# A transformer-and-SSD pipeline on one core: norms written by feature pairs, and the value projection moved to the front of its group

## What is computed

```python
# layer 2, its end
h = rms_norm(x, mlp_norm[1]);  x = x + (relu(h @ w_in) ** 2) @ w_out        # "mlp1", hidden width 4096
# hybrid layer
sh1, sc1, g1, sh2, sc2, g2 = split(silu(c) @ ada_w + ada_b, 6)              # and sh1c, sc1c from c_ctx
h  = rms_norm(x,   norm1_w) * (1 + sc1)  + sh1                              # "hx"
hc = rms_norm(ctx, norm1_w) * (1 + sc1c) + sh1c                             # "hc", 256 context tokens
p  = h @ w_in            # columns: q, k, v, z (512 each), xs 512, bc 512, dt 16
kvc, sc_in = hc @ w_in[:, 512:1536], hc @ w_in[:, 2048:]
# rope on q and k, neighbourhood attention with the context's keys and values,
# convolution and SSD scan of xs, B, C with dt, gated by silu(z)
x = x + g1 * (concat(attn, y_ssd) @ w_out_2)                                # "out"
h = rms_norm(x, norm2_w) * (1 + sc2) + sh2                                  # "m2"
x = x + g2 * ((silu(conv(h @ up_gate)) * (h @ up_val)) @ w_down)            # "glu", 22 tiles of 128
return rms_norm(x, final_norm_w)
```

## Time and profile before

| | |
|---|---|
| median of 3 runs | 1223.09 us (1213.04 to 1224.58) |
| profiled execution, its own time | 1223.84 us |
| its span in the trace | 1221.7 us |
| TensorE matmul busy | 1077.3 us, 88% |
| VectorE busy | 734.6 us, 60% |
| ScalarE busy | 538.5 us, 44% |
| mean granted TensorE clock | 0.923 of full |

### The profile page before, as it was taken

One profiled execution on the slowest core, in us unless ns is written; L12 is line 12 of the kernel. 1 busy time (PEld: TensorE's weight loads), 2 busy tenths in 40 slices (PEclk: granted clock), 3 DMA queues, 4 the chain that ended last, 5 costly groups with the idle time before them and its releaser, 6 DMA issues.

```text
span 1221.7 us, 15756 instructions
## 1 busy us (share of the span) xinstructions
PE 1077.3 (88%) x6140; PEld 923.2 (76%) x6140; DVE 734.6 (60%) x996; ACT 538.5 (44%) x726; POOL 96.9 (8%) x71
## 2 busy tenths in 40 slices
PE   3786899998998988999999979898889677999995
PEld 2574689888887866889999769776436567999994
DVE  5556566898745555757766555532456546566564
ACT  3455446564424555544555326323332034444442
POOL 0002002675000010000000000000000000000000
PEclk8878999999989998999999979988786688999998
DMA  4343256676732551457776412420100042545431
GB/s 163 105 141 105 81 212 235 237 270 230 257 142 104 183 195 69 172 207 272 280 277 236 175 70 75 143 104 24 73 1 1 1 155 91 195 164 205 174 152 52
DMA packets 29007, 184.05 MB, mean 151 GB/s; under 512 B 3472, under 2 KB 5008, under 8 KB 9360
## 3 DMA queue, kind: packets, MB, share of 16 engines
q1 hardware_dynamic: 23360, 153.82, 34.4%
q0 software_dynamic: 3456, 25.17, 5.7%
q10 hardware_dynamic: 2144, 4.42, 1.5%
HBM read 180.77 MB, written 2.62 MB: 150 GB/s over the span
## 4 chain that ended last, share of the span: by engine, by line
PE 52%; issue 21%; DVE 13%; ACT 6%; DMA 1%; POOL 1%; DVEq 0%; POOLq 0%; ACTq 0%; SPq 0%
PE bank L579 13%; PE bank L580 13%; PE bank L581 13%; DVE split L1548 4%; ACT split L1081 4%; PE bank L588 2%; PE bank L1007 2%; PE bank L981 2%; PE bank L965 1%; PE bank L807 1%; DMA raw<-w_mlp 1%; PE bank L993 1%; POOL stat L518 1%; PE bank L744 1%; ACT work L1137 1%
## 5 line engine op out<-in xcount | busy, mean ns | idle before, releaser
L1548 DVE TENSOR_TENSOR split<-raw,split 128x2048 fp32r<-128x2048 f32 (+2 forms) x133 | 300.0, 2256 | 293.8 <-ACT split L1081 288.2
L1081 ACT ACTIVATE split<-raw 128x2048 fp32r<-128x2048 f32 (+2 forms) x133 | 247.6, 1862 | 352.3 <-PE bank L581 306.2
L579 PE MATMUL bank<-acts,split 128*128 128x256 f32 (+1 forms) x1024 | 292.3, 285 | 12.6 <-DVE acts L1578 12.3
L580 PE MATMUL bank<-acts,split 128*128 128x256 f32 (+1 forms) x1024 | 291.7, 285 | 0.0
L581 PE MATMUL bank<-acts,split 128*128 128x256 f32 (+1 forms) x1024 | 291.5, 285 | 0.0
L579 PE MATMUL bank<-split,acts 128*128 128x512 f32 (+3 forms) x616 | 245.0, 398 | 39.4 <-DVE split L1548 13.2
L580 PE MATMUL bank<-split,acts 128*128 128x512 f32 (+3 forms) x616 | 239.9, 389 | 0.0
L581 PE MATMUL bank<-split,acts 128*128 128x512 f32 (+3 forms) x616 | 239.5, 389 | 0.0
L579 PEld LDWEIGHTS bank<-acts,split 128*128 128x128 f32 (+1 forms) x1024 | 196.4, 192 | 16.6 <-DVE acts L1578 13.1
L580 PEld LDWEIGHTS bank<-acts,split 128*128 128x128 f32 (+1 forms) x1024 | 196.3, 192 | 2.5
L581 PEld LDWEIGHTS bank<-acts,split 128*128 128x128 f32 (+1 forms) x1024 | 196.2, 192 | 0.7
(11 more groups left out here) (225 smaller groups left out, 1168.4 us busy)
## 6 DMA issues: line engine op xcount, KB each, us to landing
raw<-w_mlp SPq DMA_DIRECT2D x64, 1024.0 KB, 4.8
raw<-w_glu SPq DMA_DIRECT2D x22, 1024.0 KB, 5.5
work<-w_ada POOLq DMA_DIRECT2D x12, 1024.0 KB, 5.2
raw<-w_qkv SPq DMA_DIRECT2D x12, 1024.0 KB, 4.8
bias<-w_ada POOLq DMA_DIRECT2D x12, 1024.0 KB, 5.1
arena<-w_glu_down SPq DMA_DIRECT2D x22, 512.0 KB, 3.3
raw<-w_mla_o SPq DMA_DIRECT2D x4, 1024.0 KB, 4.7
raw<-w_moba_o SPq DMA_DIRECT2D x4, 1024.0 KB, 4.8
```

The costliest lines, as they stand in the source:

```text
L579: pe.matmul(out_, a[0], b[0], start=first, stop=False)
L580: pe.matmul(out_, a[0], b[1], start=False, stop=False)
L1081: return act.activation(out_, in_, ACT.Copy)
L1548: v.tensor_tensor(split[:, c % 2, 1, 0:n], raw[:, c % 2, 0:n], split[:, c % 2, 0, 0:n].bitcast(F32), ALU.subtract).then_inc(lo_ready, 1)
```

## The change

1. **Feature pairs.** For hc, hx and m2 the transposes are grouped so that a bank holds two features of all 256 tokens (`pairs_to_cols`), for which both token tiles must be there. The modulation of a bank is then two `tensor_scalar` operations of 128x256, each multiplying and adding with a per-partition gain and shift (`two_values`), in place of two spread operations of 128x512. High and low parts are made by pairs (`two_hi`, `two_lo`).
2. **The context beside the second MLP.** Its transposes are issued after n = 27 in place of n = 30, its scaling after n = 28, its first two high copies at n = 28, first two low parts at n = 30. The banks are taken in the order 2, 3, 0, 1 (`HC_ORDER`). The unit numbers are moved so that hc has the four units behind up 14, and up 15 the one behind those (`up_step`).
3. **v first.** v is the first projection; its chunks are stored in reverse, so that features 4 to 7 come first. The context's rows of the first chunk stand before the transposes of hx, those of the second chunk behind them, then x's rows. Chunk v1 is split by VectorE before hx is modulated.
4. **The first up-step of the gated MLP** starts feature pair by feature pair (`first_up` with 2 tiles and 1 unit).

```diff
@@ GEMMS
-         ("dt", 1, 1, 1), ("xs", 2, 4, 1), ("bc", 2, 4, 1), ("q", 2, 2, 2), ("k", 2, 6, 1), ("z", 2, 2, 2),
-         ("v", 2, 4, 2), ("out", 4, 4, 2), ("glu", 22, 22, 1)]
+         ("v", 2, 4, 2), ("dt", 1, 1, 1), ("xs", 2, 4, 1), ("bc", 2, 4, 1), ("q", 2, 2, 2), ("k", 2, 6, 1), ("z", 2, 2, 2),
+         ("out", 4, 4, 2), ("glu", 22, 22, 1)]
+def up_step(name, step):
+    return step + 4 if (name, step) == ("mlp1", 15) else step
@@ plan()
         if name == "mlp1":
-            first_unit["ada1"], first_unit["hc"] = unit, unit + 3
+            first_unit["ada1"], first_unit["hc"] = unit + 4, unit - 1
+HC_ORDER = (2, 3, 0, 1)
@@ TensorE
+            def pairs_to_cols(name, norm):
+                for t in range(2):
+                    pe.wait_ge(x_normed[t], norm)
+                for n in range(4):
+                    flip(SU[name] + n, [(T * a + P * t, xn[:, t, (2 * n + a) * P:(2 * n + a + 1) * P])
+                                        for a in range(2) for t in range(2)])
...
-                if n == 30:
+                if n == 27:
                     pe.wait_ge(normed, 4)
-                    for t in range(2):
-                        for half in range(2):
-                            flip(GU["hc"] + 2 * t + half,
-                                 [(P * f, ctx[:, t, (4 * half + f) * P:(4 * half + f + 1) * P]) for f in range(4)], True)
+                    for m in range(4):
+                        flip(GU["hc"] + m, [(T * a + P * t, ctx[:, t, (2 * m + a) * P:(2 * m + a + 1) * P])
+                                            for a in range(2) for t in range(2)], True)
             mlp("mlp1", "m1", 16, 2, 3, modulation_and_context)
-            rows_to_cols("hx", 1)
+            def values(c, which):
+                for t in range(2):
+                    n = GU["v"] + t + (0 if which else 2)
+                    if c == 0:
+                        gemm_start(n)
+                    for k in range(4):
+                        ins = product(gbank(n)[:, :], act_pair(which, 4 * (1 - c) + k, t * P, P),
+                                      tuple(p[:, k, :] for p in slot(GC["v"] + c, 4, 512)),
+                                      c == 0 and k == 0, c == 1 and k == 3)
+                    if c:
+                        ins.then_inc(gemm_ready, 1)
+                if c == 0 and not which:
+                    ins.then_inc(down_used, 1)
+            weights_in(GC["v"])
+            pe.wait_ge(act_lo, LO["hc"] - 2)
+            values(0, 1)
+            pairs_to_cols("hx", 1)
+            weights_in(GC["v"] + 1)
+            pe.wait_ge(act_lo, LO["hc"])
+            values(1, 1)
             pe.wait_ge(act_lo, LO["hx"])
+            values(0, 0)
+            values(1, 0)
...
-            rows_gemm("v", 2, 4, 512, 512, both, 2)
...
-            rows_to_cols("m2", 2)
-            pe.wait_ge(act_lo, LO["m2"])
+            pairs_to_cols("m2", 2)
...
+                if i is None and s == 0:
+                    first_up(GC["glu"], GU["glu"], "m2", 2, 1)
+                    return
@@ ScalarE
-            square_relu("mlp1")
+            def context_values(n, i=None):
+                if i is None and n == 28:
+                    for m in HC_ORDER[:2]:
+                        two_hi("hc", m, 1)
+            square_relu("mlp1", context_values)
             x_squares(SU["d1"], range(4), True)
-            cols_hi("hc", 1)
+            for m in HC_ORDER[2:]:
+                two_hi("hc", m, 1)
             norm_second_tile(11)
-            cols_hi("hx")
             used(GC["mlp1"] + 31)
+            modulated_hi("hx")
@@ VectorE
+                    ins = v.tensor_scalar(value_of(name, n, a, 1), (gbank if which else sbank)(u)[:, T * a:T * (a + 1)],
+                                          gain[:, f:f + 1], shift[:, f:f + 1], ALU.mult, ALU.add)
...
+                if n == 28:
+                    for m in HC_ORDER:
+                        two_values("hc", m, adac[:, 64:72], adac[:, 32:40], 1)
                 if n == 30:
-                    for m in range(4):
-                        cols_scale("hc", m, adac[:, 64:72], adac[:, 32:40], True)
+                    for m in range(2):
+                        two_lo("hc", HC_ORDER[m], HI0["hc"] + m + 1, 1)
...
-            cols_out("hx", adac[:, 48:56], adac[:, 0:8])
             used(GC["mlp1"] + 31)
+            modulated_lo("hx", adac[:, 48:56], adac[:, 0:8])
```

More of the change, by code:

```diff
@@ L102, in plan @@
                 if not is_down:
-                    released.append(("gemm", unit + step + 1))
+                    released.append(("gemm", unit + up_step(name, step) + 1))
                 elif step < n // 2 - 1:
@@ L413, in place, with two_of, value_of @@
             return (4 * (n // 2), n % 2) if name in RAW else (4 * (n % 2), n // 2)
+        def two_of(which, part_, n):
+            return acts[:, which, part_, 2 * n * T:(2 * n + 2) * T]
+        def value_of(name, n, a=0, m=2):
+            at = (0 if name == "hx" else 2048) + 512 * n + T * a
+            return att[:, at:at + T * m]
         def tokens_of(which, part_, k, t):
```

69 lines of the change are left out of this document (47 added, 22 removed).

## The result

Over 14 runs each, the changed kernel took 1209.23 us in the median (1206.05 to 1216.21), the kernel before 1220.59 us (1213.04 to 1224.98). The ratio is 0.9913 with a 95% interval of 0.9891 to 0.9936: 10.6 us less, give or take 2.8. The forecast was 1216 us, in a range of 1207 to 1227, and 7.0 us of gain. So the time lies in the range, and the change comes out at the very edge of what 1% can tell. The forecast of the time is 6.8 us too high: 2.5 us of that is its base, since over 14 runs the kernel before has a median of 1220.6 and not the 1223.1 of its first three, and the rest is gain that was not forecast. The sum behind it was right in most of its terms and lacked one.

What follows compares the result with a forecast made beforehand. TensorE was taken to bound the kernel, with 23 us of waits for VectorE to earn from. Terms -10.4 + 11.0 + 6.4 gain 7.0 us: 1223.84 less 7.0, less 0.75 for the median, gives 1216 us, range 1207 to 1227.

Steps and rivals of the forecast that it cites:

- Part 1: Context's transposes inside the second MLP: the last four wait for ScalarE's Relu on up 14's bank, a loss of 1.4 us.
- Part 2: Second MLP: up 15 waits for bank 2, released by VectorE's sixth scaling behind a weight split, a loss of 6.8 us.
- Part 3: Up 15 in the second MLP: TensorE runs at half clock after the long wait, a loss of 2.2 us.
- The rival of the cold clock: Second MLP onward: TensorE stays at half clock through up 15, down 14 and second context product; 1229 us, chance 0.14.
- the quicker alternative: Context scalings before up 15: were PSUM operations as quick as the SBUF row, the wait would be 0.8 us shorter.
- Part 4: From the second MLP's last matmul to dt's end: v's context products fill the norm's time, a gain of 11.0 us.
- Part 5: Behind z, where v stood: nothing more gained or lost; 7.7 us of slack, running sums' 3.51 us wait stays.
- Part 6: Norm before the gated MLP: earlier first up-step and kept clock gain 6.4 us; 2.11 us gap before first down-step stays.
- The clock does not come back: Rival: half clock lasts through up 15, down 14 and second context product, last norm yields 5.1; 1229 us, chance 0.14.
- v was a cover: Rival: behind z TensorE waits for VectorE's backlog, up to 21.9 us come back; 1238 us, chance 0.05.
- The clock holds everywhere: Rival: neither up 15 nor the context product loses much clock, last norm gives 7.3 us; 1212 us, chance 0.16.
- The change doesn't do what it says: Rival: the norm's time is not filled, since v1's split comes late, giving 6 us, not 11; 1221 us, chance 0.05.

## Why the prediction was right, and where it wasn't

**Parts 1 to 3, the MLP: 10.4 us forecast, about 12.2 measured.** From the U of before to E it was 31.0 us with the transposes in it, and 43.2 us from the transposes to E after. Part 1: 1.18 us for 1.4. Part 2: 7.13 us for 6.8; each scaling took 0.45 us from start to start where 0.40 was taken, and six make the 0.3. Part 3: up 15 took 7.4 us where 48 matmuls at full clock take 5.75, so 1.7 us for 2.2. What was left out is the modulation behind up 15: +1.8 us. The rival of the cold clock named its light matmuls, but the sum had no term for them.

The Trainium skill's rule that an fp32 operation with a PSUM operand stays at the single rate (VectorE: DVE Perf Modes, "Why PSUM operands drop a tier"), weighed in Part 2, is borne out against the quicker alternative. The eight scalings out of banks took 3.70 us together, none near the 0.353 us of the row on SBUF.

**Part 4, the norm's time: 11.0 us forecast, 10.8 measured** (38.9 us of path less 28.1). Every step held within 0.4 us, and the kernel with the norm's time left empty gave the same amount back, 10.6 us by the times and 9.1 to 10.7 in the trace. The clock loss behind the second gap was 1.6 us for 1.2: 72 matmuls took 18.07 us, at full clock 16.4.

Parts 1 to 4 were to gain 0.6 us together. By these steps they lost 1.4 us; up to the sums the two traces differ by 0.6, since the projections from dt to z took 0.8 us less. Against the other two profiles of before it is 2 and 4 us, since there the old joint was cheaper. How much the joint lost can't be told from one profile: the joint of before varies by 3.8 us over its three.

**Part 5, "nothing more": the step that failed.** It was right in what it looked at: no gap stands behind z, and the wait for the running sums is 3.51 us as before. But it looked for waits alone and put the clock behind z at nothing. With v gone from there, the stretch behind it took 124.0 to 124.4 us in nine profiles, where with v there it took 131.7 to 133.2 in four of five: 7 to 9 us, by its clock. The change's net gain at the MLP and the norm is nothing; what made the kernel with all but the last norm 2.8 us faster than before is this stretch, whose 7.9 us (132.3 less 124.4) stand against a joint that lost 0.6 to 4. These trace figures would give 3.5 to 7.3 us, and the interval reaches to 5.4. Executions of before with the cheap attention, as the one caught with only the last norm changed, would bring the times closer still. How often before has them stays open: its three profiles, of 1221.6 to 1224.1 us, all have the dear one, but of 60 executions of before that were timed beside the other kernels 12 took 1211.2 to 1215.4 us and 48 took 1217.4 or more. The twelve lie about where 8 us less would put them, and none of them was profiled.

**Part 6, the last norm: 6.4 us forecast, 7.5 measured from the first transpose to the first down-step.** From yT to the second down-step the table gives 5.0 to 7.9 us. The 2 us by which the kernels with this norm differ there are largely given back behind it: from yT to the end of the span it is 243.1 to 243.8 us in the nine profiles with the changed norm and 250.3 to 251.2 in the four with the old one, so 6.5 to 8.1 us. The first up-step started 3.77 us behind the first transpose (3.7), the second 10.96 (11.0). What was mis-sized is the last sentence: the gap of 2.11 us before the first down-step was to stay, and it shrank to 0.73. The trace with the up-step waiting for all shows it: there the gap is 2.11 again, behind an up-step that ran cold. The forecast also gave the early start and the kept clock 5.1 and 2.2 us as separate gifts; the run shows that without the early start the pairs alone give nothing that the trace or the times can tell.

**The rivals.** "The clock does not come back" fell: up 15 was back within its length, down 14 and 15 took 13.2 us in both kernels. "v was a cover" fell: no gap. "The clock holds everywhere" gave the time nearest to the measurement, 1212, and not by its own mechanism: clock was lost in up 15, in the modulation and in the second value product. It was gained behind z, where the forecast had no term. "The change doesn't do what it says" fell with Part 4.

So the forecast held with luck. In the paired traces the missing term of the attention's clock gave 7.3 us and the last norm 0.7 more than its term (7.1 from yT to the second down-step), the joint lost 0.6 where 0.6 was to be gained, and the untouched code ahead took 3.0 us longer: 7.0 + 7.3 + 0.7 - 1.2 - 3.0 = 10.8, with 10.9 between the two spans.

## What to carry to other kernels

When work is moved into an engine's queue, ask not only how long it takes but what it stands behind: eight ready scalings behind one split that wasn't cost 7 us of waiting and 4 more of clock, and one step earlier they cost no wait.

Filling a wait pays through the clock too, here some 4 us on 7; at the last norm the shorter chain alone showed nothing, and the early start that kept TensorE at work was worth all of it.

Compare two traces over stretches that the change does not touch as well, by landmarks and with one window over each; a median of a whole kernel puts such a gain down to the edit that one has in mind.

## What was not expected of the hardware

The same 389 matmuls, with 24.4 to 25.0 us of idle time between them in all 14 profiles, took 98.0 to 99.5 us in ten profiles and 107.3 to 108.7 us in four. The granted clock was 0.78 to 0.79 in the ten and 0.71 to 0.73 in the four. The windows from the first matmul of this stretch on, 60 us of before and of after:

```profile
839.65:899.65 60.00, 48.43 (x171) 28.21 (x171) 26.85 (x66) 25.55 (x51) 0.00 (x0) 0.77 0.10 38
899.65:971.39 71.74, 58.89 (x219) 42.61 (x217) 43.30 (x109) 15.31 (x28) 0.70 (x1) 0.69 0.00 1
```
```profile
843.28:903.28 60.00, 47.95 (x193) 29.13 (x193) 29.48 (x72) 27.26 (x55) 0.00 (x0) 0.89 0.10 38
903.28:967.71 64.43, 51.58 (x198) 39.14 (x196) 40.57 (x102) 12.66 (x22) 0.69 (x1) 0.68 0.00 1
```

The difference arises in the first 60 us, in which after got 193 matmuls done and before 171; behind them both have about the same clock. Inside them it is where the attention begins. In before, 16 us of it ran at 0.57, in after the same part ran at full clock:

```profile
867.60:883.60 16.00, 14.68 (x32) 6.26 (x32) 7.86 (x19) 5.94 (x15) 0.00 (x0) 0.57 0.22 92
```
```profile
863.30:895.30 32.00, 26.26 (x111) 13.53 (x109) 19.94 (x55) 15.75 (x36) 0.00 (x0) 1.00 0.18 70
```

The matmuls that before did in those 16 us took 8.7 us in after (872.92 to 881.62). One stretch at half clock marks all four dear profiles: it begins 29.5 to 30.9 us behind the sums and lasts 13.7 us, and none of the ten cheap ones has any half clock there. In before:

```profile
869.20:882.90 13.70, 13.70 (x31) 5.93 (x30) 6.29 (x16) 4.04 (x10) 0.00 (x0) 0.50 0.14 58
```

Half of 13.7 us is 6.9, most of the difference. The stretch takes either 122.9 to 124.4 or 131.7 to 133.2 us, and nothing between. Which of the two is not decided by the clock's level at its start: the 4 us ahead of the sums were at full clock in all three profiles of before, in after, and in both profiles with only the last norm changed, the cheap one and the dear one. It goes with what ran further back: in the old order 96 matmuls of v without a gap stand directly ahead of the sums, in the new one z with a gap of 2.38 us, 8 to 10 us ahead of them. That this decides is not shown: no run changed the work ahead of the sums with the rest kept, and the one cheap profile in the old order had v there too. The Trainium skill (TensorE: Matmul & The Clock Gate, "What's actually happening") says that the number of slow matmuls at a kernel's start varies from run to run, and holds the loss for less than 1% of a typical kernel. What varies here lies in the middle of the kernel: the joint of before by 3.8 us, and this one stretch, which alone is worth 0.6% and in 13 of 14 profiles went with the program's order.

The modulation's 36 matmuls, 32 of them one column wide, took 4.9 us at a clock of 0.99 and 6.7 at 0.73. Behind the wait of 7.13 us it was 6.6 to 6.7 in four profiles and 5.9 in one. But without any gap before up 15 it was 4.9 in four profiles, 5.1 in two, and 6.5 and 6.6 in two more. So the wait brings the slow case nearly always, and it comes without the wait too. Up 15 and the modulation belong together: in the six profiles with a wait before up 15 (7.13 us, once 5.32) they took 14.0 to 14.1 us in sum, and where the modulation was quicker, 5.9 and 5.8 us, up 15 was slower, 8.1 and 8.2 in place of 7.4 to 7.5.
